# The last output tile of a two-block transformer layer: its second half shared by two engines

## The chip, the cores and the metric

The kernel runs on one core of a Trainium2 chip. A core has five engines that run their own instruction streams and meet only through semaphores: TensorE (PE, matrix products), VectorE (DVE, elementwise work), ScalarE (ACT, activations), GpSimd (POOL, elementwise work and its own DMA queue) and SyncE (SP, which here issues DMAs). Sixteen DMA engines move data between the core's memory (SBUF) and DRAM. The metric is the device time of one execution in microseconds (us); the median of several runs counts.

## The reference

Two transformer blocks follow each other on 512 tokens of 1024 channels. The change touches only the last lines of the second block: the product of the feed-forward network with its down matrix, its norm, and the residual.

```python
def rms_norm(x, g):
    xf = x.astype(jnp.float32)
    y = xf * lax.rsqrt(jnp.mean(xf * xf, axis=-1, keepdims=True) + RMS_EPS)
    return (y * g.astype(jnp.float32)).astype(x.dtype)
...
        f = jax.nn.gelu(u_gate, approximate=True) * u_val
        y = f @ w_down[layer].astype(f.dtype)
        x = x + rms_norm(y, norm_ffn_post[layer])
    return x
```

## The kernel before

Nearly all of the time goes into matrix products in three passes of split operands (`whi`, `wlo` for weights, `xh`, `xl` or `fh`, `fl` for activations). SyncE streams 270 weight pieces through four slots; ScalarE rounds each to `whi`, VectorE takes the rest `wlo`. The last phase, `down2`, computes its output by token rows: `QB` = 4 tiles of `P` = 128 tokens, each with two halves of `SEQ` = 512 channels, so that eight banks of PSUM hold tile t, half h at bank 2t+h. TensorE (`down_rows`, L745) runs the first 19 of the 22 weight pieces for all eight banks, and the last three bank by bank, so that the banks are finished one after another, about 2 us apart; each raises `rows_done`.

Behind TensorE stands a chain for each tile t:

- ScalarE (`rows_rooted`, L1174) squares a bank and sums the squares along a row into `row_sums`, and raises `rows_squared`. After the second half it takes the root of the mean (`row_root`, L1184).
- VectorE (`rows_out`, L1642) scales the first half's sum (`row_bias`, L1651), multiplies each bank by the gains into `gained` (L1653), inverts the root into `row_inv` (L1655), and finishes each half with one SCALAR_TENSOR_TENSOR (L1659): `gained * row_inv + res_rows`, where `res_rows` is the residual in row form. Each raises `rows_ready`. `step` counts a semaphore `vstep` at the end of an instruction, and `after_step` waits until all counted ones have ended.
- SyncE (L456 to L461) waits for each half in turn, stores it (256 KB), and at the end waits until all eight stores have landed (`stored`).

GpSimd has no part in this phase: its last work is a list of DMA issues that prepare `res_rows` and `gain_rows` (L520 to L527). All eight stores go through SyncE's queue. The order of all this is written out by hand.

Of the kernel before, what the change touches and what calls it, by code (L numbers as in the profile page):

```python
# [19 lines left out]
D = 1024  # L20
KD = D // P
SEQ = 512
# [15 lines left out]
QB = SEQ // P  # L38
# [123 lines left out]
KEPT_WHOLE = KFF - 3  # L162
TURN_ITS = (4, 5, 6, 7)
T_FROM = 18
BIAS_W = 384
STAT = 4
SUMS_AT = 496
# [15 lines left out]
def two_block_kernel(nc, x_in, w_in, vec_in, gain_in, dftc_in, dftp_in, onehot_in, rel_in, out):  # L183
    F32, F32R = mybir.dt.float32, mybir.dt.float32r
    ALU = mybir.AluOpType
# [4 lines left out]
    with ExitStack() as ctx:  # L190
        def sem(name):
            return ctx.enter_context(nc.semaphore(name))
# [42 lines left out]
        row_root = put("row_root", [P, QB])  # L235
        row_inv = put("row_inv", [P, QB])
# [37 lines left out]
        gained = put("gained", [P, QB, D], offset=x_at)  # L274
        turned = [put(f"turned{n}", [P, SEQ // 64, KD, 32], offset=big + (n * KFF + T_FROM) * SEQ * 4) for n in range(2)]
        res_rows = put("res_rows", [P, QB, 4, D // 4], offset=res_at)
# [106 lines left out]
        row_bias_ready = sem("row_bias_ready")  # L383
        row_root_ready = sem("row_root_ready")
        rows_ready = sem("rows_ready")

        def vec(name, n):
            return vecs[:, VCOL[name] + n:VCOL[name] + n + 1] if isinstance(n, int) else vecs[:, ds(n + VCOL[name], 1)]
# [50 lines left out]
        @block.sync  # L439
        def _(sp):  # L440
            sp.dma_start(vecs[:, 0:KD], vec_in[:, 0:KD]).then_inc(gain_landed, 16)
            for k in range(KD):
                sp.dma_start(res[:, k, :], x_in[:, k, :]).then_inc(x_landed[k], 16)
                if k % 2 == 0:
                    sp.dma_start(raw[:, k // 2, :], w_in[k // 2]).then_inc(w_landed[k // 2], 16)
            sp.dma_start(vecs[:, KD:], vec_in[:, KD:]).then_inc(vec_landed, 16)
            with sp.Fori(1, CHUNKS // SLOTS_W) as it:
                for s in range(SLOTS_W):

                    sp.wait_ge(w_used, it * SLOTS_W + (s - SLOTS_W + 1))  # L450
                    sp.dma_start(raw[:, s, :], w_in[ds(it * SLOTS_W + s, 1)].rearrange("a p c -> (a p) c")) \
                      .then_inc(w_landed[s], 16)
            for n in range(CHUNKS // SLOTS_W * SLOTS_W, CHUNKS):
                sp.wait_ge(w_used, n - SLOTS_W + 1)
                sp.dma_start(raw[:, n % SLOTS_W, :], w_in[n]).then_inc(w_landed[n % SLOTS_W], 16)
            for t in range(QB):  # L456
                for h in range(2):
                    sp.wait_ge(rows_ready, 2 * t + h + 1)
                    sp.dma_start(out[t, :, h * SEQ:(h + 1) * SEQ], gained[:, t, h * SEQ:(h + 1) * SEQ]) \
                      .then_inc(stored, 16)  # L460
            sp.wait_ge(stored, 32 * QB)  # L461


        @block.gpsimd
        def _(pool):
            pool.memset(ones[:, :], 1.0).then_inc(set_up, 1)
            pool.memset(ident[:, :], 0.0).then_inc(set_up, 1)
            pool.memset(folded[:, :, :, :], 0.0).then_inc(set_up, 1)
            pool.memset(cin1[:, :, 0:1], 0.0).then_inc(set_up, 1)
            pool.memset(cin1[:, :, N1 + 1:N1 + 2], 0.0).then_inc(set_up, 1)  # L470
            pool.memset(stage[:, :, N1:N1 + 2], 0.0).then_inc(set_up, 1)
            pool.memset(small[:, 2:3], RMS_EPS).then_inc(set_up, 1)
            pool.memset(small[:, 3:4], LN_EPS).then_inc(set_up, 1)
            pool.wait_ge(set_up, 2)
            pool.affine_select(out=ident[:, :], in_=ident[:, :], compare_op=ALU.not_equal, fill=1.0, base=0,
                               pattern=[[-1, P]], channel_multiplier=1).then_inc(set_up, 1)
            pool.wait_ge(x_landed[KD - 1], 16)
            pool.dma_start(onehot[:, :, :], onehot_in).then_inc(onehot_landed, 16)
            pool.dma_start(rel[:, :], rel_in).then_inc(onehot_landed, 16)

            pool.wait_ge(bias_copied, NG)
            for g in range(NG):
                pool.dma_start(bias_dram[g * HEADS:(g + 1) * HEADS, :],
                               bias_rows[g * HEADS:(g + 1) * HEADS, g, :]).then_inc(bias_stored, 16)
            pool.dma_start(dftp[0:ROWS, :, :, :], dftp_in).then_inc(dft_landed, 16)
            pool.dma_start(dftc, dftc_in).then_inc(dft_landed, 16)

            pool.wait_ge(bias_stored, 16 * NG)
            for n in range(NG * HEADS):
                if n:  # L490
                    pool.wait_ge(bias_spread, 16 * n)
                pool.dma_start(bias_copies[n], bass.AP(bias_dram.tensor, n * BIAS_W, [[0, P], [1, BIAS_W]])) \
                    .then_inc(bias_spread, 16)
            pool.wait_ge(bias_spread, 16 * NG * HEADS)

            def load_bias(j):

                for g in range(NG):
                    c0, c1 = ((0, 256), (256, 384), (384, 512))[g]
                    pool.dma_start(  # L500
                        bias[:, c0:c1],
                        bass.AP(bias_copies.tensor, (g * HEADS + j) * P * BIAS_W + P - 1,
                                [[BIAS_W - 1, P], [1, c1 - c0]])).then_inc(bias_landed, 16)

            for j in range(HEADS):
                if j:
                    pool.wait_ge(max_ready, 2 * j)
                else:
                    pool.wait_ge(operand_ready, READY["x2"])
                load_bias(j)  # L510
                pool.wait_ge(exp_ready, 8 * (j + 1))
                for kind in range(2):
                    pool.dma_start(stats_rows(kind == 0, 2 * SEQ * kind), head_stats[:, 0, 4 * kind:4 * kind + 4, :]) \
                        .then_inc(stats_stored, 16)
                pool.wait_ge(stats_stored, 32 * (j + 1))
                for kind in range(2):
                    pool.dma_start(head_stats[:, 1, 4 * kind:4 * kind + 4, :],
                                   stats_rows(kind == 0, 2 * SEQ * (1 - kind))).then_inc(stats_landed, 16)

            pool.wait_ge(res_turned, 2 * KD)  # L520
            for a in range(4):
                for u in range(4):
                    for n in range(2):
                        pool.dma_start(res_rows[32 * u:32 * (u + 1), 2 * n:2 * n + 2, a, :],
                                       turned[n][32 * a:32 * (a + 1), :, :, :]
                                       .rearrange("p (t u) c i -> p t u (c i)", u=4)[:, :, u]).then_inc(res_moved, 16)
            pool.dma_start(gain_rows[:, :], bass.AP(gain_in.tensor, 0, [[0, P], [1, D]])).then_inc(gain_spread, 16)  # L527


        @block.tensor  # L530
# [482 lines left out]
        def _(act):  # L1013
# [400 lines left out]
                          lambda k: xh2[:, k, :])  # L1414
            ffn_gelus("up2")
            rows_rooted("down2")


        @block.vector
        def _(dve):  # L1420
            steps = [0, 0]

            def step(instruction):
                instruction.then_inc(vstep, 1)
                steps[1] += 1

            def after_step():

                dve.wait_ge(vstep, steps[0] + steps[1])
# [212 lines left out]
            def rows_out():  # L1642
                for n in range(3, KFF):
                    w_to_lo("down2", 0, n)
                dve.wait_ge(gain_spread, 16)
                for t in range(QB):
                    for h in range(2):
                        cols = slice(h * SEQ, (h + 1) * SEQ)
                        dve.wait_ge(rows_squared, 2 * t + h + 1)
                        if h == 0:  # L1650
                            dve.tensor_scalar(row_bias[:, t:t + 1], row_sums[:, t, 0:1], 1.0 / D, RMS_EPS,  # L1651
                                              ALU.mult, ALU.add).then_inc(row_bias_ready, 1)
                        step(dve.tensor_tensor(gained[:, t, cols], ps[:, 2 * t + h, :], gain_rows[:, cols], ALU.mult))  # L1653
                    dve.wait_ge(row_root_ready, t + 1)
                    step(dve.reciprocal(row_inv[:, t:t + 1], row_root[:, t:t + 1]))  # L1655
                    after_step()
                    for h in range(2):
                        cols = slice(h * SEQ, (h + 1) * SEQ)
                        dve.scalar_tensor_tensor(out=gained[:, t, cols], in0=gained[:, t, cols],  # L1659
                                                 scalar=row_inv[:, t:t + 1],  # L1660
                                                 in1=res_rows[:, t, :, :].rearrange("p a n -> p (a n)")[:, cols],
                                                 op0=ALU.mult, op1=ALU.add).then_inc(rows_ready, 1)

            def down_sums(dn, name):
# [510 lines left out]
```

## Time and profile before

| what | us |
|---|---|
| median of 3 runs | 1582.26 |
| lowest and highest run | 1581.83, 1583.42 |
| the profiled execution | 1582.33 |
| its span, from first to last instruction | 1580.5 |
| TensorE busy in the span | 1570.8 |
| VectorE, ScalarE, GpSimd busy | 1103.5, 557.0, 47.3 |

The span is what the trace shows; the profiled execution's own time is 1.83 us longer. All times of single instructions are counted from the span's start. In the timeline a row gives start, duration, engine, line, operation, what it writes and reads, and in brackets how long the engine was idle before and who released it. Instructions of one engine can overlap by some hundredths of a microsecond, since the next may be taken in before the last has drained.

### The profile page before, as it was taken

The page shows a single profiled execution, that of the slowest core. Times are in us where ns is not written, and L with a number is a line of the kernel's source. Part 1 is how long each engine was busy: PE and PEld are TensorE (multiplying, and loading weights), DVE is VectorE, ACT ScalarE, POOL GpSimd, SP SyncE. Part 2 cuts the span into 40 slices and gives each one's busy share as a digit, 9 for nine tenths or more (in the row PEclk, how much of TensorE's full clock was granted, in tenths as well). Part 3 has the DMA queues.
Part 4 walks back from the last instruction along what each step waited for, and adds up shares of the span by engine and source line. Part 5 has one row for each costly group of instructions (what it writes and reads, how often), then busy time and mean ns, then how long its engine had stood idle before and what let it go on. Part 6 is the DMA issues. An engine that isn't in the chain of part 4 may idle for free.

```text
span 1580.5 us, 24351 instructions
## 1 busy us (share of the span) xinstructions
PE 1570.8 (99%) x9542; PEld 1417.9 (90%) x9542; DVE 1103.5 (70%) x1594; ACT 557.0 (35%) x809; POOL 47.3 (3%) x93
## 2 busy tenths in 40 slices
PE   9999999999999999999999999999999999999998
PEld 9999999999999988998889898888889888888887
DVE  6334456689888853278999898974656899988224
ACT  5123333542222222254234444458335422222112
POOL 1110000000000000000001010000000000040000
PEclk9999999999999999999999999999999999999999
DMA  5443222233333233333333232322332333363332
GB/s 175 115 137 93 87 70 86 79 95 93 93 93 88 87 105 107 94 103 92 101 99 87 80 101 74 94 82 80 96 102 70 107 94 98 101 159 93 102 98 93
DMA packets 44793, 154.18 MB, mean 98 GB/s; under 512 B 6346, under 2 KB 6374, under 8 KB 44720
## 3 DMA queue, kind: packets, MB, share of 16 engines
q1 hardware_dynamic: 41472, 146.21, 30.5%
q0 software_dynamic: 3248, 6.93, 2.0%
q8 instruction: 53, 0.87, 0.2%
q14 instruction: 20, 0.16, 0.0%
HBM read 148.88 MB, written 4.51 MB: 97 GB/s over the span
## 4 chain that ended last, share of the span: by engine, by line
PE 89%; DVE 8%; ACT 1%; DMA 1%; issue 1%; SPq 0%; DVEq 0%
PE ps L539 65%; PE ps L741 8%; PE ps L549 7%; PE ps L914 4%; DVE wlo L1444 2%; PE ps L577 1%; DVE work L1845 1%; DVE work L1570 1%; DVE work L1573 1%; PE ps L965 1%; DMA raw<-w_dram 1%; DVE work L1605 1%; DVE stage L1561 1%; PE ps L854 1%; DVE fl L1619 0%
## 5 line engine op out<-in xcount | busy, mean ns | idle before, releaser
L539 PE MATMUL ps<-xh,whi 128*128 128x258 f32 (+2 forms) x1800 | 495.2, 326 | 1.1 <-DVE stage L1566 0.8
L539 PE MATMUL ps<-xh,wlo 128*128 128x258 f32 (+2 forms) x1800 | 490.6, 323 | 0.0
L539 PE MATMUL ps<-xl,whi 128*128 128x258 f32 (+2 forms) x1800 | 489.9, 323 | 0.0
L1018 ACT ACTIVATE whi<-raw 128x1024 fp32r<-128x1024 f32 x270 | 285.3, 1058 | 476.4 <-DMA raw<-w_dram 454.7
L1444 DVE TENSOR_TENSOR wlo<-raw,whi 128x1024 fp32r<-128x1024 f32 x270 | 329.1, 1219 | 171.7 <-ACT whi L1018 171.1
L539 PEld LDWEIGHTS ps<-xh,whi 128*128 128x128 f32 x1800 | 301.5, 189 | 29.0 <-issue 3.4
L539 PEld LDWEIGHTS ps<-xh,wlo 128*128 128x128 f32 x1800 | 300.7, 189 | 27.1
L539 PEld LDWEIGHTS ps<-xl,whi 128*128 128x128 f32 x1800 | 301.4, 189 | 25.7 <-issue 0.2
L1845 DVE SCALAR_TENSOR_TENSOR work<-cin,vecs,work 128x512 f32<-128x512 f32 x240 | 180.1, 751 | 6.9
L1566 DVE TENSOR_TENSOR stage<-ps,rstd 128x516 f32<-128x516 f32 x57 | 39.5, 694 | 64.5 <-PE ps L539 62.2
L1573 DVE SCALAR_TENSOR_TENSOR work<-stage,vecs,work 128x512 f32<-128x512 f32 x88 | 66.2, 752 | 7.5 <-DVE work L1570 0.5
L1570 DVE SCALAR_TENSOR_TENSOR work<-stage,vecs,work 128x512 f32<-128x512 f32 x88 | 66.1, 752 | 7.5 <-DVE work L1605 0.5
L741 PE MATMUL ps<-whi,fl 128*128 128x512 f32 x176 | 68.5, 389 | 0.0
L741 PE MATMUL ps<-whi,fh 128*128 128x512 f32 x176 | 68.5, 389 | 0.0
L741 PE MATMUL ps<-wlo,fh 128*128 128x512 f32 x176 | 68.5, 389 | 0.0
L1144 ACT ACTIVATE work<-work 128x512 f32<-128x512 f32 x44 | 27.8, 631 | 103.4 <-DVE work L1573 103.2
L539 PE MATMUL ps<-fl,whi 128*128 128x512 f32 x132 | 51.4, 389 | 0.0
L539 PE MATMUL ps<-fh,wlo 128*128 128x512 f32 x132 | 51.4, 389 | 0.0
L539 PE MATMUL ps<-fh,whi 128*128 128x512 f32 x132 | 51.4, 389 | 0.0
L1605 DVE TENSOR_SCALAR work<-stage,vecs 128x512 f32<-128x512 f32 x88 | 47.7, 543 | 0.2
L549 PE MATMUL ps<-xh,whi 128*128 128x256 f32 (+1 forms) x160 | 45.9, 287 | 0.2 <-DVE xl L1480 0.2
L549 PE MATMUL ps<-xh,wlo 128*128 128x256 f32 (+1 forms) x160 | 45.2, 283 | 0.0
(255 smaller groups left out, 2292.4 us busy)
## 6 DMA issues: line engine op xcount, KB each, us to landing
raw<-w_dram SPq DMA_DIRECT2D x270, 512.0 KB, 3.5
bias_copies_dram<-bias_rows_dram POOLq DMA_DIRECT2D x12, 192.0 KB, 3.8
res<-x_dram SPq DMA_DIRECT2D x8, 264.0 KB, 6.2
res_rows<-turned POOLq DMA_DIRECT2D x32, 64.0 KB, 3.3
out_dram<-gained SPq DMA_DIRECT2D x8, 256.0 KB, 2.0
dftp<-dftp_dram POOLq DMA_DIRECT2D x1, 550.7 KB, 4.5
bias<-bias_copies_dram POOLq DMA_DIRECT2D x4, 128.0 KB, 2.8
bias<-bias_copies_dram POOLq DMA_DIRECT2D x8, 64.0 KB, 3.1
```

What stands on the lines that cost most here:

```text
L539: last = pe.matmul(ps[:, bank, 0:b - a], w[:, slot, cols], xx[:, k, a:b], start=start and n == 0, stop=stop and n == 2)
L549: last = pe.matmul(ps[:, bank, at_:at_ + b - a], w[:, slot, cols], xx[:, k, a:b], start=start and n == 0, stop=stop and n == 2)
L741: last = pe.matmul(ps[:, 2 * t + h, :], f[:, k, rows], w[:, slot, cols], start=k == k0 and n == 0, stop=k == k1 - 1 and n == 2)
L914: last = pe.matmul(ps[:, TILE_BANK[t], :], xx[:, 2 * c + k2, rows], w[:, n % 4, k2 * SEQ:(k2 + 1) * SEQ], start=c == 0 and k2 == 0 and m = ...
L1018: act.activation(whi[:, slot, :], raw[:, slot, :], ACT.Copy).then_inc(w_hi, 1)
L1144: act.activation(work[:, 1, 0:SEQ], work[:, 0, 0:SEQ], ACT.Gelu_apprx_tanh) \
L1444: dve.tensor_tensor(wlo[:, slot, :], raw[:, slot, :], whi[:, slot, :].bitcast(F32), ALU.subtract).then_inc(w_split, 1)
L1566: dve.tensor_tensor(halves(dst), tile_psum(slot, True), halves(by), ALU.mult).then_inc(tile_read, 1)
L1570: step(dve.scalar_tensor_tensor(out=dst, in0=src(at_, width), scalar=vec(w, tile), in1=dst, op0=ALU.mult, op1=ALU.add))
L1573: last(dve.scalar_tensor_tensor(out=dst, in0=src(at_ + 2, width), scalar=vec(w, tile + 2 * tiles), in1=dst, op0=ALU.mult, op1=ALU.add))
L1605: step(dve.tensor_scalar(row, stage[:, s, off + 1:off + 1 + SEQ], vec(w, m + (s * KFF + 2 * KFF)), vec(b, m + s * KFF), ALU.mult, ALU.add))
L1845: ins = dve.scalar_tensor_tensor(out=dst, in0=src, scalar=vec("conv_dw_w_2", t * KD + m), in1=dst, op0=ALU.mult, op1=ALU.add)
```

## The change

It concerns the last token tile (t = 3). Its second half, columns 512 to 1023, is cut at column 832. VectorE finishes the first half as before and then 320 columns. GpSimd finishes the last 192 (`TAIL_W`) in two instructions, a scaling by `row_inv` and an addition of `res_rows`. ScalarE's queue stores these 192 columns; SyncE stores seven halves and the 320 columns. Three semaphores are new: `tail_ready` (the reciprocal has ended), `tail_scaled` and `tail_added` (GpSimd's two steps).

```diff
+TAIL_W = 192
+STORES = [(t, h * SEQ, (h + 1) * SEQ) for t in range(QB) for h in range(2)][:-1] + \
+    [(QB - 1, SEQ, D - TAIL_W)]
...
-            for t in range(QB):
-                for h in range(2):
-                    sp.wait_ge(rows_ready, 2 * t + h + 1)
-                    sp.dma_start(out[t, :, h * SEQ:(h + 1) * SEQ], gained[:, t, h * SEQ:(h + 1) * SEQ]) \
-                      .then_inc(stored, 16)
-            sp.wait_ge(stored, 32 * QB)
+            for n, (t, a, b) in enumerate(STORES):
+                sp.wait_ge(rows_ready, n + 1)
+                sp.dma_start(out[t, :, a:b], gained[:, t, a:b]).then_inc(stored, 16)
+            sp.wait_ge(stored, 16 * len(STORES) + 16)
...
+            pool.wait_ge(tail_ready, 1)
+            t, last = QB - 1, slice(D - TAIL_W, D)
+            pool.tensor_scalar(gained[:, t, last], gained[:, t, last], row_inv[:, t:t + 1], None, ALU.mult) \
+                .then_inc(tail_scaled, 1)
+            pool.wait_ge(tail_scaled, 1)
+            pool.tensor_tensor(gained[:, t, last], gained[:, t, last],
+                               res_rows[:, t, :, :].rearrange("p a n -> p (a n)")[:, last], ALU.add) \
+                .then_inc(tail_added, 1)
...
             rows_rooted("down2")
+            act.wait_ge(tail_added, 1)
+            act.dma_start(out[QB - 1, :, D - TAIL_W:D], gained[:, QB - 1, D - TAIL_W:D]).then_inc(stored, 16)
...
                     dve.wait_ge(row_root_ready, t + 1)
-                    step(dve.reciprocal(row_inv[:, t:t + 1], row_root[:, t:t + 1]))
-                    after_step()
-                    for h in range(2):
-                        cols = slice(h * SEQ, (h + 1) * SEQ)
-                        dve.scalar_tensor_tensor(out=gained[:, t, cols], in0=gained[:, t, cols],
+                    if t == QB - 1:
+                        after_step()
+                        dve.reciprocal(row_inv[:, t:t + 1], row_root[:, t:t + 1]).then_inc(tail_ready, 1)
+                        dve.wait_ge(tail_ready, 1)
+                    else:
+                        step(dve.reciprocal(row_inv[:, t:t + 1], row_root[:, t:t + 1]))
+                        after_step()
+                    for _, a, b in [store for store in STORES if store[0] == t]:
+                        dve.scalar_tensor_tensor(out=gained[:, t, a:b], in0=gained[:, t, a:b],
                                                  scalar=row_inv[:, t:t + 1],
```

VectorE's last instructions before the change, the last tile's chain at the end of the program (each row: line, operation, output and inputs, shape, and the semaphores it waits for):

```order
L1651 TENSOR_SCALAR row_bias<-row_sums 128x1 [waits rows_squared]
L1653 TENSOR_TENSOR gained<-ps,gain_rows 128x512
L1653 TENSOR_TENSOR gained<-ps,gain_rows 128x512 [waits rows_squared]
L1655 RECIPROCAL row_inv<-row_root 128x1 [waits row_root_ready]
L1659 SCALAR_TENSOR_TENSOR gained<-gained,row_inv,res_rows 128x512 [waits vstep]
L1659 SCALAR_TENSOR_TENSOR gained<-gained,row_inv,res_rows 128x512
```

The same instructions with the change:

```order
L1665 TENSOR_SCALAR row_bias<-row_sums 128x1 [waits rows_squared]
L1667 TENSOR_TENSOR gained<-ps,gain_rows 128x512
L1667 TENSOR_TENSOR gained<-ps,gain_rows 128x512 [waits rows_squared]
L1671 RECIPROCAL row_inv<-row_root 128x1 [waits vstep,row_root_ready]
L1677 SCALAR_TENSOR_TENSOR gained<-gained,row_inv,res_rows 128x512 [waits tail_ready]
L1677 SCALAR_TENSOR_TENSOR gained<-gained,row_inv,res_rows 128x320
```

The wait on `vstep` has moved ahead of the reciprocal, the first half waits for `tail_ready`, and the last instruction has 320 columns.

GpSimd's last instructions with the change, behind its DMA issues (before, its program ends with the issue of `gain_rows`):

```order
L528 DMA res_rows<-turned_98 32x2x256
L528 DMA res_rows<-turned_99 32x2x256
L531 DMA gain_rows<-gain_dram 128x1024
L534 TENSOR_SCALAR gained<-gained,row_inv 128x192 [waits tail_ready]
L537 TENSOR_TENSOR gained<-gained,res_rows 128x192 [waits tail_scaled]
```

Two instructions are added at the end, each behind its own wait, and nothing on GpSimd is queued behind them.

## Rows read from the trace of the kernel before

**Rows 1.** The page: span, TensorE's busy time, the chain by engine.

```profile
span 1580.5 us, 24351 instructions
PE 1570.8 (99%) x9542; PEld 1417.9 (90%) x9542; DVE 1103.5 (70%) x1594; ACT 557.0 (35%) x809; POOL 47.3 (3%) x93
...
PE 89%; DVE 8%; ACT 1%; DMA 1%; issue 1%; SPq 0%; DVEq 0%
```

**Rows 2.** Timeline of the end: start, us, engine, line, operation, [idle before].

```profile
1574.75 0.39 PE L741 MATMUL ps<-wlo,fh 128*128 128x512 f32 x1
1575.17 0.60 ACT L1180 ACTIVATE sq<-ps 128x512 f32<-128x512 f32 x1 [1.35 <-PE ps L741]
1575.67 0.20 ACT L1180 ACTIVATION_READ_ACCUMULATOR sq<-ps 128x1 f32 x1
1575.89 0.29 ACT L1184 ACTIVATE row_root<-row_sums,row_bias 128x1 f32<-128x1 f32 x1
1575.89 0.69 DVE L1653 TENSOR_TENSOR gained<-ps,gain_rows 128x512 f32<-128x512 f32 x1 [1.21 <-ACT sq L1180]
1576.50 0.15 DVE L1655 RECIPROCAL row_inv<-row_root 128x1 f32<-128x1 f32 x1
1576.69 1.42 DVE L1659 SCALAR_TENSOR_TENSOR gained<-gained,row_inv,res_rows 128x512 f32<-128x512 f32 x2
```

**Rows 3.** Timeline of VectorE from 1577.5 on: the second half alone.

```profile
1577.36 0.75 DVE L1659 SCALAR_TENSOR_TENSOR gained<-gained,row_inv,res_rows 128x512 f32<-128x512 f32 x1
```

**Rows 4.** Timeline of SyncE's queue: issues of the last two stores.

```profile
1577.47 0.33 SPq L459 DMA_DIRECT2D out_dram<-gained  x1
...
1578.13 0.33 SPq L459 DMA_DIRECT2D out_dram<-gained  x1
```

**Rows 5.** The stores' line (ns of an issue, landing) and SyncE's last wait.

```profile
L459 SPq DMA_DIRECT2D out_dram<-gained x8: 332/333/344, 1565.2 to 1578.1; - x8
...
DMA to landing us min/median/max: 2.0/2.0/2.0
...
SPq L190 <- DMA out_dram<-gained: 1.7, 1, 1.7
```

**Rows 6.** Stretches: us, each engine's busy time, granted clock, DMA share, GB/s.

```profile
1578.20:1578.30 0.10, 0.00 (x0) 0.00 (x0) 0.00 (x0) 0.00 (x0) 0.00 (x0) 1.00 0.00 0
1578.30:1578.40 0.10, 0.00 (x0) 0.00 (x0) 0.00 (x0) 0.00 (x0) 0.00 (x0) 1.00 0.87 348
1578.90:1579.00 0.10, 0.00 (x0) 0.00 (x0) 0.00 (x0) 0.00 (x0) 0.00 (x0) 1.00 0.67 246
...
1579.70:1579.80 0.10, 0.00 (x0) 0.00 (x0) 0.00 (x0) 0.00 (x0) 0.00 (x0) 1.00 0.03 0
...
1578.20:1579.80 1.60, 0.00 (x0) 0.00 (x0) 0.00 (x0) 0.00 (x0) 0.00 (x0) 1.00 0.85 328
```

**Rows 7.** Groups on VectorE by shape: count, busy us, mean ns, idle before.

```profile
L1573 DVE SCALAR_TENSOR_TENSOR work<-stage,vecs,work 128x512 f32<-128x512 f32 x88 | 66.2, 752 | 7.5 <-DVE work L1570 0.5
...
L1480 DVE SCALAR_TENSOR_TENSOR xl<-res,vecs,xh 128x256 fp32r<-128x256 f32 x16 | 7.6, 477 | 0.4 <-ACT xh L1115 0.4
...
L1659 DVE SCALAR_TENSOR_TENSOR gained<-gained,row_inv,res_rows 128x512 f32<-128x512 f32 x8 | 5.7, 749 | 0.1
```

**Rows 8.** Timeline of GpSimd at the program's start.

```profile
0.25 0.10 POOL L2165 MEMSET const-float32-0.0<- 128x1 f32 x1 [0.25 <-issue]
...
0.75 0.20 POOL L466 MEMSET ones<- 128x128 f32 x1 [0.29 <-POOLq L2165]
...
2.98 0.10 POOL L473 MEMSET small<- 128x1 f32 x1
3.11 0.28 POOL L475 TENSOR_SCALAR_AFFINE_SELECT ident<-ident 128x128 f32<-128x128 f32 x1
```

**Rows 9.** GpSimd's issues; DMAs with KB and us to landing; a stretch of copies.

```profile
L524 POOL DMA_DIRECT2D res_rows<-turned x32 | 17.1, 544 | 347.3 <-DVE turned L1638 347.3
...
vecs<-vec_dram SPq DMA_DIRECT2D x1, 4.0 KB, 1.7
...
1399.00:1400.00 1.00, 1.00 (x7) 0.81 (x6) 0.96 (x3) 0.39 (x1) 1.00 (x3) 1.00 0.49 119
```

More of the change, by code:

```diff
@@ L385, in two_block_kernel @@
         rows_ready = sem("rows_ready")
+        tail_ready = sem("tail_ready")
+        tail_scaled = sem("tail_scaled")
+        tail_added = sem("tail_added")
         def vec(name, n):
@@ L1654, in rows_out @@
                     dve.wait_ge(row_root_ready, t + 1)
-                    step(dve.reciprocal(row_inv[:, t:t + 1], row_root[:, t:t + 1]))
-                    after_step()
-                    for h in range(2):
-                        cols = slice(h * SEQ, (h + 1) * SEQ)
-                        dve.scalar_tensor_tensor(out=gained[:, t, cols], in0=gained[:, t, cols],
+                    if t == QB - 1:
[7 more added lines that the diff above has]
+                        dve.scalar_tensor_tensor(out=gained[:, t, a:b], in0=gained[:, t, a:b],
                                                  scalar=row_inv[:, t:t + 1],
-                                                 in1=res_rows[:, t, :, :].rearrange("p a n -> p (a n)")[:, cols],
+                                                 in1=res_rows[:, t, :, :].rearrange("p a n -> p (a n)")[:, a:b],
                                                  op0=ALU.mult, op1=ALU.add).then_inc(rows_ready, 1)
```

## The prediction

> **What bounds the kernel now.** I began with the page's busy line and its chain [rows 1]: TensorE is busy for 1570.8 of 1580.5 us and carries 89% of the chain that ended last. The change touches none of its instructions and nothing before the last token tile. So the question is only what happens after the last matmul, and I read that stretch from the timeline [rows 2]. The last matmul is started at 1574.75 and ScalarE's square of the last bank starts at 1575.17. VectorE then multiplies the last bank by the gains (1575.89, 0.69 us), inverts the root (1576.50, 0.15 us), and finishes the two halves with two SCALAR_TENSOR_TENSOR, the first from 1576.69, the second from 1577.36 [rows 3]. SyncE issues the store of the first half at 1577.47 and that of the second at 1578.13 [rows 4]; each lands 2.0 us after its issue, and the last wait is 1.7 us for a store [rows 5]. The span closes at 1580.5.
>
> The view that decides is the stretch of the stores [rows 6]. The DMA engines are idle until 1578.3, 0.83 us after the first issue. They are then close to full until 1579.7: over 1.6 us they are busy 0.85, which is 1.36 us of work, inside 1.4 us of wall time. The share dips once, to 0.67 at 1578.9, where the second store takes over from the first. Each store is thus about 0.68 us of work for all engines, and the second begins when the first is drained, which happens to be 0.84 us after its own issue (1578.13 + 0.84 = 1578.97). Two limits lie on each other here: VectorE's second half, and the drain of 512 KB, which starts with the first half's store. Shortening VectorE's second half alone moves only the first of the two.
>
> **The scale.** The span's 1580.5 us belong to a run of 1582.33 us, 1.83 us outside the span; that run lies 0.07 us over the median of 1582.26 us. The runs are spread over 1.6 us. About 0.2%, 3.2 us, is what a measurement of this kernel can tell from no change. Everything from the end of the reciprocal (1576.65) to the end of the span is 3.85 us, and the part that the change rewrites, the two halves on VectorE, is 1.42 us of it. No outcome of the sharing itself can be a gain of 3.2 us.
>
> **The change, part by part.** First, the reciprocal of the last tile now waits for VectorE's own last product. Before, it started at 1576.50, ahead of the product's end at 1575.89 + 0.69 = 1576.58 [rows 2]. Behind this wait on VectorE stand the reciprocal and both halves; SyncE and GpSimd wait for those. A step behind a wait on its predecessor starts 0.04 us after it here (reciprocal ends at 1576.65, the half starts at 1576.69), so the reciprocal starts at 1576.62, 0.12 us later. The other bound is the convolution's chain of such steps, 7.5 us of idle time before 88 of them [rows 7], 0.085 us each: 1576.67, 0.17 us later. I take 0.12, since its row is the same place. The first half then starts at 1576.81 and ends at 1577.56, and its store is issued at 1577.59 in place of 1577.47.
>
> Second, VectorE's second half shrinks from 512 to 320 columns. The same instruction takes 749 ns with 512 columns and 477 ns with 256 [rows 7], or 1.06 ns per column; 320 columns give 477 + 64 x 1.06 = 545 ns, 204 ns less. It starts, as before, 0.08 us ahead of the end of the first (1577.48) and ends at 1578.02, where 1578.11 stood. VectorE's gain is thus 0.20 - 0.12 = 0.08 us. SyncE's issue of the first store ends at 1577.59 + 0.33 = 1577.92, ahead of this, so the queue is no limit; the second store is issued at 1578.05.
>
> Third, GpSimd takes 192 columns in two instructions, a scaling and an addition, each behind a semaphore. The trace of before has no such instruction. The nearest rows are its memsets, 98 ns with 1 column and 205 ns with 128, and its select, which reads and writes 128 columns, 282 ns [rows 8]. By the memset a column costs 0.84 ns, so 192 cost 0.26 us; by the select 1.45 ns, so 0.38 us. That bounds the scaling. The addition reads two tensors: its lower bound is the select's 0.38 us, its upper bound twice the select's price per column, 0.66 us. Between dependent instructions GpSimd shows 0.03 us (3.08 to 3.11). So from tail_ready at 1576.77: start 1576.80, end between 1577.5 and 1577.9. The row that it is nearest to is the select, so I take the upper half, 1577.8. None of it lies on the path yet: VectorE's halves run until 1578.02 beside it, and the next point says how long the cover holds.
>
> Fourth, ScalarE issues the 96 KB of those columns. Its last work, the root, ends at 1576.18; nothing is queued behind its wait. An issue takes 0.33 us on SyncE [rows 5] and 0.54 us on GpSimd's queue [rows 9], and the data start 0.83 us after the start of an issue: with the columns ready at 1577.8, about 1578.7. The engines are then still draining the first store, from 1578.42 to 1579.10. The other two stores are 160 KB and 96 KB, 0.42 and 0.25 us of work. If the 160 KB go first, the 96 KB are needed at 1579.52, so ScalarE may issue as late as 1578.69 before the end moves. This is GpSimd's cover: 0.9 us beyond my 1577.8, and 0.8 us beyond its upper bound.
>
> Fifth, the drain. The bytes are the same 512 KB, and their start is 0.12 us later. A single queue's two stores already keep the engines full [rows 6]; no row shows two hardware queues storing at once. The Trainium skill's page "DMA: Bandwidth & Descriptors", section "Issuing engines are not separate DMA queues", states that DMAs of any issuing engine end on the same 16 DMA engines, and that several issuers only save issue time; by it the drain stays 1.36 us of work, and were it otherwise the 0.25 us of the tail store could be hidden. The rows give the same choice without it: full engines have nothing to give. What is dearer is that each row of 2 KB now leaves in two pieces, 1280 and 768 bytes. From below this costs nothing: work in proportion to bytes. From above, a stretch in which mostly 1 KB pieces move (64 KB copies between tiles) runs at 119 GB/s with a share of 0.49 [rows 9], 243 GB/s if full, 67 ns a piece, against 328/0.85 = 386 GB/s and 85 ns for a 2 KB piece of the stores. A straight line through both gives 62 and 71 ns for the two pieces, 48 ns more per row, and with 128 rows on 16 engines 8 x 48 ns = 0.38 us. Those copies go between tiles and through another queue, while the stores are their own nearest row, so I take 0.10 us, nearer to the lower bound.
>
> **The sum.** End of drain: 1579.70 + 0.12 + 0.10 = 1579.92; receipt and close as before, so the span is 1580.7 and the run 1582.33 + 0.22 = 1582.55. Taken back to the median (0.07) this is 1582.5 us. With the bounds, +0.10 to +0.55: 1582.4 to 1582.8. This is no change that can be measured.
>
> **Rival one: GpSimd and VectorE take turns, slower.** Both halves on VectorE read two tensors in SBUF, and both GpSimd instructions read SBUF. No row shows the two engines so at the same time. If they exclude each other, their times add up whatever the order: on VectorE 1.21 us for both halves, on GpSimd 0.26 to 0.38 and 0.38 to 0.66 us, with three handovers of 0.03 us, 1.95 to 2.35 us from 1576.81, so the last of them ends at 1578.75 to 1579.15. If GpSimd's addition is last, ScalarE issues 0.1 to 0.5 us after the latest harmless time, 1578.69. If GpSimd goes first, the first half's store starts 0.26 to 0.38 us later, and the drain with it. Added to the forecast's 0.22, this is 0.3 to 0.7 us, middle 0.5: 1582.8 us. It decides from the point at which GpSimd's sum is finished after 1578.69. The Trainium skill's page "SBUF — State Buffer", section "Who interferes with whom", states this exclusion for a VectorE instruction with two SBUF inputs against a GpSimd instruction that reads SBUF, as a lock held for the whole instruction. Against it stands no row, for it none either: its chance is 0.32.
>
> **Rival two: the last issue is the limit, faster.** All eight stores land 2.0 us after issue, the last of a pair as well as the first [rows 5], and 4 KB on the same queue land in 1.7 us [rows 9]. If landing goes by the issue and the size of the last store, not by the drain, then SyncE's last store (issued at 1578.05, 0.08 us earlier) lands between 0.08 and 0.38 us earlier, middle 0.25: 1582.0 us. The full engines of rows 6 speak against it. Chance 0.14.
>
> **Rival three: something is paid once, slower.** GpSimd does its first arithmetic since 3.1 us into the span, and ScalarE's queue its first transfer. GpSimd's first instruction stands 0.25 us after the start, its select follows the memset by 0.03 us [rows 8], and SyncE's first transfers show no price of this kind. So by rows it is 0 to 0.25 us, hidden in GpSimd's cover of 0.9. It shows in the time only from 0.9 us on, and in a measurement only from some 4 us on. The Trainium skill's page "GPSIMD Engine Reference", section "Instruction dispatch", gives about 6 us for the first call of a freshly loaded kernel; were that due here, the estimate would be 1582.5 + 5 = 1587.5 us. Chance 0.04.
>
> **How the numbers follow.** Forecast 1582.5 us with 0.50, rival one 1582.8 with 0.32, rival two 1582.0 with 0.14, rival three with 0.04. The first three are all within 3.2 us of the median, so "same" gets 0.95; a little under the third rival, 0.04, goes to slower and 0.01 to faster, for which the profile has no mechanism. The range leaves out rival three and the outer part of the others. The cases' own bounds run from 1581.9 to 1583.0; the spread of the runs, 1581.83 to 1583.42, adds about half a microsecond on either side: 1581.4 to 1583.6.
>
> **What would show it.** In the timeline after: the reciprocal right behind the product (1576.62 in the times of before), not ahead of its end; a half of 320 columns at about 0.545 us; GpSimd's two instructions, whose lengths and place beside VectorE's halves tell the forecast from rival one (stretched halves, or GpSimd idle until a half ends, show exclusion). In the DMA windows: a start 0.12 us later relative to the last matmul, and 1.36 to 1.75 us of work. If the last transfer to land is ScalarE's, GpSimd's cover was too small. The forecast is wrong if the close of the span follows the last issue by less than before, or if a run differs by more than 3 us, which would mean a cost that these rows do not hold.

## The result, and the profile after

The changed kernel takes 1587.70 us (median of 7 runs, 1587.15 to 1589.47) against 1582.26 us before: the ratio is 1.0035, 95% interval 1.0025 to 1.0045. It is slower by 5.4 us, and the prediction of 1582.5 us, in a range to 1583.6, was wrong.

The loss is all behind VectorE's last product. The page's head, and the timeline from VectorE's last product on (columns as in [rows 2]):

```profile
span 1585.8 us, 24355 instructions
PE 1569.7 (99%) x9542; PEld 1416.6 (89%) x9542; DVE 1103.7 (70%) x1594; ACT 557.2 (35%) x809; POOL 49.5 (3%) x95
...
1575.91 0.69 DVE L1667 TENSOR_TENSOR gained<-ps,gain_rows 128x512 f32<-128x512 f32 x1 [1.20 <-ACT sq L1192]
1576.70 0.16 DVE L1671 RECIPROCAL row_inv<-row_root 128x1 f32<-128x1 f32 x1
1576.90 1.38 DVE L1677 SCALAR_TENSOR_TENSOR gained<-gained,row_inv,res_rows 128x512 f32<-128x512 f32 x2
1576.97 1.32 POOL L534 TENSOR_SCALAR gained<-gained,row_inv 128x192 f32<-128x192 f32 x1 [161.56 <-DVE row_inv L1671]
1577.68 0.96 SPq L464 DMA_DIRECT2D out_dram<-gained  x2
1578.38 0.59 POOL L537 TENSOR_TENSOR gained<-gained,res_rows 128x192 f32<-128x192 f32 x1
1579.00 0.37 ACTq L1430 DMA_DIRECT2D out_dram<-gained  x1
```

VectorE's last product starts at 1575.91 where 1575.89 stood [rows 2], so up to there nothing has changed. From there to the end of the span it was 4.61 us; now it is 9.89 us. The last issue, ScalarE's, is at 1579.00, and its 96 KB land 1.8 us later, at 1580.8. Five more microseconds pass in which this timeline shows nothing.

They are seen in the rows of the program's end. Line 193 (190 before) is the `with` under which all engines' programs stand; each engine's closing steps carry its number. Some of these rows, first before, then after (x and count, ns of one as minimum/median/maximum, first and last start):

```profile
L190 POOLq DRAIN  x1: 10122/10122/10122, 1412.8 to 1412.8; - x1
L190 SPq COMPARE_BRANCH  x1: 38/38/38, 1580.2 to 1580.2; - x1
L190 SPq DRAIN  x1: 7/7/7, 1580.3 to 1580.3; - x1
```

```profile
L193 POOLq EVENT_SEMAPHORE  x2: 17/17/17, 1585.6 to 1585.7; - x2
...
L193 DVEq DRAIN  x1: 1420/1420/1420, 1576.9 to 1576.9; - x1
L193 POOLq DRAIN  x1: 7257/7257/7257, 1578.3 to 1578.3; - x1
L193 ACTq DRAIN  x1: 147/147/147, 1579.4 to 1579.4; - x1
L193 SPq COMPARE_BRANCH  x1: 38/38/38, 1580.8 to 1580.8; - x1
L193 SPq DRAIN  x1: 7/7/7, 1581.0 to 1581.0; - x1
L193 SPq EVENT_SEMAPHORE  x1: 17/17/17, 1585.8 to 1585.8; - x1
```

Each engine closes its program with an instruction that the trace names DRAIN, and then the engines meet at semaphores. GpSimd's DRAIN takes microseconds. Before, GpSimd reached its end behind its DMA issues at 1412.8 and its 10.1 us lay under the products of the last weights. Now it begins when the addition has been started (1578.34, the last piece of the chain of work below), lasts 7.26 us to 1585.6, and the program ends right behind it. SyncE's waits show the same from the other side (us in total, times, longest); before, its wait on line 190 for the meeting was 0.2 us:

```profile
1576.97 1.32 POOL gained L534
1578.29 0.04 issue
1578.34 0.63 POOLq L193
...
SPq L193 <- PEq L193: 4.8, 1, 4.8
SPq L193 <- DMA out_dram<-gained: 2.1, 1, 2.1
```

So of the 5.3 us in the trace, 0.6 us are a later last landing (SyncE's DRAIN starts at 1580.96, before at 1580.32, which the rows round to tenths: 5.05 us behind the product's start, 4.42 before) and 4.6 us are SyncE's longer wait for the meeting. The waits name PE, which was long done (its own drain began at 1570.9); the one late engine among the closing rows is GpSimd.

### The profile page after: what moved, and what is told of

It reads as the page before. It is cut to its first block, busy times and chain, and to the rows that moved or that the text cites. A ratio compares the mean times of both kernels' runs of the same rounds, so it can differ in the third digit from the quotient of the medians.

```text
span 1585.8 us, 24355 instructions
## 1 busy us (share of the span) xinstructions
PE 1569.7 (99%) x9542; PEld 1416.6 (89%) x9542; DVE 1103.7 (70%) x1594; ACT 557.2 (35%) x809; POOL 49.5 (3%) x95
## 4 chain that ended last, share of the span: by engine, by line
PE 89%; DVE 8%; ACT 1%; DMA 1%; issue 1%; POOL 0%; SPq 0%; POOLq 0%; DVEq 0%
PE ps L551 65%; PE ps L753 8%; PE ps L561 7%; PE ps L926 4%; DVE wlo L1458 2%; PE ps L589 1%; DVE work L1863 1%; DVE work L1584 1%; DVE work L1587 1%; PE ps L977 1%; DMA raw<-w_dram 1%; DVE work L1619 1%; DVE stage L1575 1%; PE ps L866 1%; DVE fl L1633 0%
## 5 line engine op out<-in xcount | busy, mean ns | idle before, releaser
L561 PE MATMUL ps<-xl,whi 128*128 128x256 f32 (+1 forms) x160 | 45.2, 283 | 0.0
```

The costliest lines, as they stand in the source:

```text
L561: last = pe.matmul(ps[:, bank, at_:at_ + b - a], w[:, slot, cols], xx[:, k, a:b], start=start and n == 0, stop=stop and n == 2)
```

## Experiments

The theory after the result: GpSimd's closing drain has a length of its own, counted from the end of its work, and whatever makes GpSimd reach its end late puts that length on the path. Its rivals: ScalarE's queue, used for the first time, closes late; or a price is paid once, by GpSimd's first arithmetic.

**Without GpSimd's part.** VectorE does the 192 columns itself, ScalarE still stores them.

```diff
-            pool.wait_ge(tail_ready, 1)
-            pool.tensor_scalar(gained[:, t, last], ...).then_inc(tail_scaled, 1)
-            pool.wait_ge(tail_scaled, 1)
-            pool.tensor_tensor(gained[:, t, last], ...).then_inc(tail_added, 1)
...
+                    if t == QB - 1:
+                        a, b = D - TAIL_W, D
+                        dve.scalar_tensor_tensor(...).then_inc(tail_added, 1)
```

> GpSimd's two instructions are taken out; VectorE finishes the 192 columns itself with a third instruction, and ScalarE's queue still stores them. Theory A (GpSimd's closing drain, 7.26 us in the changed kernel, is the loss): the drain is back at 1413 us, hidden, and what is left is the later reciprocal and one more VectorE instruction (192 columns, about 0.33 us on the path): span 1580.8 us, time 1582.6. Rival (ScalarE's queue, used for the first time, is what closes late): span stays at 1585 us.

Measured: 1582.60 us, ratio 1.0003 (0.9994 to 1.0013). Closing rows, and VectorE's parts alone:

```profile
L193 POOLq DRAIN  x1: 10239/10239/10239, 1412.5 to 1412.5; - x1
L193 ACTq DRAIN  x1: 147/147/147, 1578.6 to 1578.6; - x1
...
1577.28 0.55 DVE L1669 SCALAR_TENSOR_TENSOR gained<-gained,row_inv,res_rows 128x320 f32<-128x320 f32 x1
1577.74 0.41 DVE L1675 SCALAR_TENSOR_TENSOR gained<-gained,row_inv,res_rows 128x192 f32<-128x192 f32 x1
```

GpSimd's drain is back under the products and the 5 us are gone, while ScalarE's queue is still in use and drains in 0.15 us. The queue is not the cause.

**The same work once before.** The changed kernel, with GpSimd's two kinds of instruction run on scratch at 1415 us.

```diff
+            pool.memset(scr[:, :], 1.0).then_inc(warm, 1)
+            pool.wait_ge(warm, 1)
+            pool.tensor_scalar(scr[:, 8:200], scr[:, 8:200], scr[:, 0:1], None, ALU.mult).then_inc(warm, 1)
+            pool.wait_ge(warm, 2)
+            pool.tensor_tensor(scr[:, 8:200], scr[:, 8:200], scr[:, 8:200], ALU.add).then_inc(warm, 1)
             pool.wait_ge(tail_ready, 1)
```

> The changed kernel, with a memset and the same two kinds of GpSimd instruction (192 columns, on scratch) once before, behind GpSimd's last DMA issue at 1415 us. Theory A1 (the drain has this length behind any late GpSimd work): span 1585.8, time 1587.7, as in the changed kernel. Rival A2 (a price paid once, by the first arithmetic): the drain at the end is short, span about 1581.2 us, time 1583.

Measured: 1587.88 us, ratio 1.0034 (1.0021 to 1.0047), and GpSimd's rows, with the instruction that VectorE ran beside the first use:

```profile
1414.99 0.75 DVE L1594 SCALAR_TENSOR_TENSOR work<-stage,vecs,work 128x512 f32<-128x512 f32 x1
1415.20 1.18 POOL L536 TENSOR_SCALAR scr<-scr 128x192 f32<-128x192 f32 x1
...
1576.36 1.32 POOL L541 TENSOR_SCALAR gained<-gained,row_inv 128x192 f32<-128x192 f32 x1 [159.40 <-DVE row_inv L1678]
...
L193 POOLq DRAIN  x1: 7255/7255/7255, 1577.7 to 1577.7; - x1
```

The scaling takes 1.32 us when it is the second of its kind, as it did in the changed kernel where it was the first: no price of the first use shows. (The first one here, 1.18 us, has VectorE beside it too and ends 0.64 us behind VectorE's instruction; what that means is read below.) The drain is 7.26 us again. Nothing of the loss is paid once.

**A bare wait.** The kernel without GpSimd's part, but GpSimd waits at its end for the last reciprocal, with no instruction behind it.

```diff
+            pool.wait_ge(tail_ready, 1)
```

> x1_no_gpsimd with a bare wait of GpSimd for the reciprocal of the last tile, and no instruction behind it. If the drain has a fixed length from the moment GpSimd reaches its end, it runs from 1576.9 for 6.6 to 7.3 us: span 1583.7 to 1584.4, time 1585.5 to 1586.2. If it is long only behind instructions that GpSimd has just run: span 1580.8 us, time 1582.6.

**One memset.** The same with a memset of one column behind the wait.

```diff
+            pool.wait_ge(tail_ready, 1)
+            pool.memset(scr[:, 0:1], 1.0)
```

> x3_wait_only with one memset of 128x1 on GpSimd behind the wait (a kind that it ran at the start, 0.1 us, no input). Drain behind any instruction: ends 6.6 us after the memset's end at 1577.1, span 1583.9, time 1585.7. Drain long only behind instructions that read SBUF, or behind first arithmetic: span 1580.8 us, time 1582.6.

Measured: 1585.99 us (ratio 1.0024, 1.0014 to 1.0033) with the bare wait, 1585.77 us (1.0023, 1.0013 to 1.0032) with the memset. The drain of the first, SyncE's wait in it, and the drain of the second:

```profile
L193 POOLq DRAIN  x1: 6602/6602/6602, 1577.2 to 1577.2; - x1
...
SPq L193 <- PEq L193: 3.2, 1, 3.2
```

```profile
1577.96 0.10 POOL L534 MEMSET scr<- 128x1 f32 x1 [161.28 <-DVE row_inv L1666]
...
L193 POOLq DRAIN  x1: 6727/6727/6727, 1577.9 to 1577.9; - x1
```

A wait alone is enough, although GpSimd had rested for 161 us. The drain is 6.60 us with nothing ahead of it; behind the memset 6.73, which is the memset's 0.10 and 6.6; in the changed kernel 7.26, which is 0.63 us until the addition has ended (1578.34 to 1578.97) and 6.63. The length of 6.6 us is the same behind a bare wait, a memset and the addition.

**The same bare wait, 3.5 us earlier.** GpSimd waits for the first finished half of tile 2 in place of the last reciprocal.

```diff
+            pool.wait_ge(rows_ready, 5)
```

> x3_wait_only, with GpSimd's bare wait moved from the last tile's reciprocal to the first finished half of the tile before (some 3.5 us earlier, at 1573.4). If the drain is 6.6 us from the moment GpSimd reaches its end, it ends at 1580.0 to 1580.1, just ahead of the last store's landing: span 1580.6 to 1580.9, time 1582.5, against 1585.99 in x3_wait_only. If a late wait of any kind costs, the time stays over 1584.

Measured: 1582.78 us (ratio 1.0002, 0.9992 to 1.0011).

```profile
L193 POOLq DRAIN  x1: 6602/6602/6602, 1573.1 to 1573.1; - x1
...
SPq L193 <- PEq L193: 0.2, 1, 0.2
```

The drain has the same 6.60 us, and now it ends at 1579.7, ahead of the last landing. What counts is when GpSimd comes to its end.

**The sharing, at another tile.** GpSimd takes the last 192 columns of tile 1 in place of tile 3, by the same instructions.

```diff
+TAIL_T = 1
...
-            t, last = QB - 1, slice(D - TAIL_W, D)
+            t, last = TAIL_T, slice(D - TAIL_W, D)
...
-                    if t == QB - 1:
+                    if t == TAIL_T:
```

> The changed kernel's sharing, applied to the second token tile (t = 1) in place of the last: the same GpSimd instructions and the same cut, some 8 us before the end; ScalarE's store of its 192 columns goes out behind its last root. GpSimd ends at about 1570.5, its drain at 1577.1, hidden. Theory A: time 1582.3 (1582.0 to 1582.8), span 1580.5. Rival (sharing itself costs some us, wherever it stands): over 1585.

Measured: 1582.88 us, ratio 1.0003 (0.9993 to 1.0012).

```profile
1569.03 1.32 POOL L534 TENSOR_SCALAR gained<-gained,row_inv 128x192 f32<-128x192 f32 x1 [153.40 <-DVE row_inv L1671]
1570.43 0.60 POOL L537 TENSOR_TENSOR gained<-gained,res_rows 128x192 f32<-128x192 f32 x1
...
L193 POOLq DRAIN  x1: 7267/7267/7267, 1570.4 to 1570.4; - x1
```

The work is the same to 0.01 us, the drain too, and the time is within the interval of no change: it is not the sharing that costs, but that it stands less than 6.6 us from the end.

**How the two engines meet at SBUF.** In the changed kernel GpSimd's scaling takes 1.32 us and ends (1578.29) with VectorE's second part (1578.28). Two more kernels ran once each; they are read for their rows, not for their times. First GpSimd's part was put behind VectorE altogether:

```diff
             pool.wait_ge(tail_ready, 1)
+            pool.wait_ge(rows_ready, 2 * QB)
```

> The changed kernel, but GpSimd also waits until VectorE has finished both parts of the last tile, so that the two never run side by side. Theory A (the engines take turns at SBUF beside each other): the scaling, 1.32 us in the changed kernel, falls to 0.26 to 0.5 us, and VectorE's 320 columns, 0.71 us there, to 0.55 us. Rival (GpSimd's scaling simply takes that long): 1.2 to 1.3 us again. Either way the drain starts late: span 1585.5 to 1586.5 us.

Then VectorE's two parts were exchanged, 320 columns first:

```diff
-STORES = [...][:-1] + [(QB - 1, SEQ, D - TAIL_W)]
+STORES = [...][:-2] + [(QB - 1, SEQ, D - TAIL_W), (QB - 1, 0, SEQ)]
```

> The changed kernel with VectorE's two parts of the last tile in the other order: 320 columns first, then 512, GpSimd's scaling beside them as before. It tells how the two engines get in each other's way. If GpSimd waits until VectorE's first instruction has ended and then runs beside the second: its scaling ends some 0.2 us earlier, 1.12 us long instead of 1.32, and VectorE's second instruction (512 columns) is the longer one by 0.16 us, 0.91 us. If GpSimd waits for both: its scaling ends with VectorE's last, 1.32 us or more, and the 512 columns take 0.75. If both are only slowed throughout: 1.32 us, and either part is longer. The close is not touched: drain 7.26 us, span 1585.5 to 1586.

Measured, with GpSimd behind VectorE:

```profile
1576.91 0.55 DVE L1678 SCALAR_TENSOR_TENSOR gained<-gained,row_inv,res_rows 128x320 f32<-128x320 f32 x1
...
1577.65 0.77 POOL L535 TENSOR_SCALAR gained<-gained,row_inv 128x192 f32<-128x192 f32 x1 [162.83 <-DVE gained L1678]
1578.50 0.59 POOL L538 TENSOR_TENSOR gained<-gained,res_rows 128x192 f32<-128x192 f32 x1
```

and with the parts exchanged:

```profile
1576.88 1.12 POOL L534 TENSOR_SCALAR gained<-gained,row_inv 128x192 f32<-128x192 f32 x1 [161.57 <-DVE row_inv L1671]
...
1577.28 0.91 DVE L1677 SCALAR_TENSOR_TENSOR gained<-gained,row_inv,res_rows 128x512 f32<-128x512 f32 x1
```

Alone the scaling takes 0.77 us. That lies between what the two theories of that run expected (0.26 to 0.5 us, and 1.2 to 1.3), and is 0.55 us less than beside VectorE. With the short part first it loses 0.35 us, 0.20 less, which is the 0.20 us by which VectorE's first instruction is shorter; and the instruction that is slowed, by 0.16 us, is VectorE's second in both orders (712 ns for 547 with 320 columns, 912 for 749 with 512). In both orders, and at the first use in the warmed kernel, GpSimd's scaling ends 0.63 to 0.64 us behind the end of the VectorE instruction that ran when it started. So these rows read as GpSimd waiting for VectorE's first instruction and then taking 0.16 us from the second. They do not fit a lock for whole instructions in both directions: on that reading VectorE's second part would have waited for most of GpSimd's 0.64 us. Both runs closed late, as expected (spans 1586.0 and 1585.5 us).

**Three pieces on VectorE.** The kernel before, with the last tile in parts of 384, 384 and 256 columns and the middle one on ScalarE's queue.

```diff
+LAST = ((0, 384), (384, 768), (768, D))
...
+                    for a, b in LAST if t == QB - 1 else ((0, SEQ), (SEQ, D)):
```

> The kernel before, without GpSimd, the last tile finished by VectorE in three pieces of 384, 384 and 256 columns in place of two halves, the middle one stored by ScalarE's queue. The first store is issued 0.14 us earlier (384 columns by 1.06 ns and the rest: 0.61 us for 0.75), the last part ends 0.1 us later. By the drain, which starts 0.14 us earlier and has the same bytes: 0.1 to 0.2 us less than before, 1582.1; by the last issue: 0.1 us more. Either is within what the runs can tell; the trace from the last product (1575.89) to the span's end, 4.61 us before, shows which.

Measured: 1582.49 us, ratio 1.0003 (0.9994 to 1.0012).

```profile
span 1580.2 us, 24353 instructions
1575.31 0.69 DVE L1661 TENSOR_TENSOR gained<-ps,gain_rows 128x512 f32<-128x512 f32 x1 [1.20 <-ACT sq L1185]
...
1577.68 0.33 SPq L465 DMA_DIRECT2D out_dram<-gained  x1
...
1577.50:1577.60 0.10, 0.00 (x0) 0.00 (x0) 0.10 (x1) 0.00 (x0) 0.00 (x0) 1.00 0.08 31
1579.10:1579.20 0.10, 0.00 (x0) 0.00 (x0) 0.00 (x0) 0.00 (x0) 0.00 (x0) 1.00 0.12 31
1579.20:1579.30 0.10, 0.00 (x0) 0.00 (x0) 0.00 (x0) 0.00 (x0) 0.00 (x0) 1.00 0.00 0
```

From the last product to the end of the span it is 4.84 us, before 4.64 (spans unrounded; the printed tenths would give 4.89 and 4.61). That is 0.2 us more, although the first store went out 1.45 us behind the product (1576.76) where it had been 1.58. The data (columns as in [rows 6]) also start earlier, and they end at the same place, 3.9 us behind the product here and before [rows 6]. The last issue is 2.37 us behind the product, before 2.24 [rows 4], and that store lands in 2.1 us, before 2.0. So in this one trace the end follows the last issue, not the start or the end of the data.

No run found a version faster than the kernel before.

## Why the prediction was wrong, point by point

**The step that failed is the third point, GpSimd's part.** It asked who waits for GpSimd's result, found ScalarE's store and a cover of 0.9 us, and put none of GpSimd's time on the path. It left out what stands behind GpSimd's last instruction: the end of its program, for which all engines wait. The row was in the trace of before (L190, 10.1 us at 1412.8), under the same line number as SyncE's last wait, which I did read [rows 5]. In its place the runs showed 6.6 us from GpSimd's last instruction, or bare wait, to the meeting; 1578.97 + 6.6 = 1585.6, and the span ends at 1585.8. The statement that no outcome of the sharing can reach 3.2 us holds for a gain only, as it was put; the loss had no such bound, and the low chance that I gave it rested on what I had looked at.

**Rival three had nearly the time (1587.5 us) by luck.** It put a one-off price ahead of GpSimd's first arithmetic. The warmed kernel (1587.88 us) shows no one-off price, and the wait alone (1585.99 us) shows that arithmetic is not needed. The 6 us that the Trainium skill's page "GPSIMD Engine Reference", section "Instruction dispatch", gives for the first call of a freshly loaded kernel do not show in these runs: the time lies behind the work, each time.

**The reciprocal's wait.** For this 0.12 us was taken, and 0.17 was the upper bound; the reciprocal now starts 0.79 us behind the product's start, before 0.61: 0.18 us.

**VectorE's parts.** 545 ns for 320 columns was right (545 to 547 ns where GpSimd does nothing beside it). Beside GpSimd it is 712 ns, so that VectorE's gain of 0.08 us became a loss: its last part ends 2.37 us behind the product's start, before 2.22.

**GpSimd's own time.** The addition, 0.38 to 0.66 us, is 0.59. The scaling, 0.26 to 0.38 us from memset and select [rows 8], is 0.77 us alone and 1.32 beside VectorE: two bounds from instructions without a scalar operand did not bound it.

**The cover, in the fourth point, did not hold either.** GpSimd's result was ready at 1578.97 in place of 1577.8, and ScalarE issued at 1579.00, behind the 1578.69 that the prediction gave as the latest harmless time. The stretches show the cost: SyncE's two stores are through by 1579.7, and ScalarE's 96 KB follow by themselves.

```profile
1579.60:1579.70 0.10, 0.00 (x0) 0.00 (x0) 0.00 (x0) 0.00 (x0) 0.00 (x0) 0.50 0.33 103
1579.70:1579.80 0.10, 0.00 (x0) 0.00 (x0) 0.00 (x0) 0.00 (x0) 0.00 (x0) 0.50 0.01 0
1579.90:1580.00 0.10, 0.00 (x0) 0.00 (x0) 0.00 (x0) 0.00 (x0) 0.00 (x0) 0.50 0.78 269
1580.20:1580.30 0.10, 0.00 (x0) 0.00 (x0) 0.00 (x0) 0.00 (x0) 0.00 (x0) 0.50 0.15 39
...
1578.50:1580.35 1.85, 0.00 (x0) 0.00 (x0) 0.00 (x0) 0.00 (x0) 0.46 (x1) 0.50 0.77 284
```

This is the 0.6 us by which the last landing is later. Without the closing drain the change would, as an estimate, have taken 1582.26 + 0.6 = 1582.9 us, inside the stated range. The price of the smaller pieces, taken as 0.10 us, was about right: the DMA engines' work is 1.85 us by 0.77, 1.42 us, before 1.36.

**Rival one, the turns.** The mechanism is there, smaller and mostly on one side: 0.55 us on GpSimd and 0.16 on VectorE. It expected a loss of 0.3 to 0.7 us, and the later last landing is 0.6 us; in part that is luck, since GpSimd's scaling is 0.77 us by itself, where this rival counted 0.38 at most. The Trainium skill's page "SBUF — State Buffer", section "Who interferes with whom", says that these two contend and calls the shared port pair an exclusive lock. GpSimd's wait agrees; a lock that GpSimd then holds against VectorE's next instruction for all of its own is not what 0.16 us shows, and the measurement decides.

**The drain of the DMA engines, and rival two.** The forecast let the last landing follow the start of the first store. The three pieces speak for rival two's reading, the last issue plus 1.8 to 2.1 us, and the kernel without GpSimd (issue 1578.18, landing 2.0 us later) fits it too. These are single traces and tenths of a microsecond, so this is likely and not shown. That rival forecast a gain since it took VectorE's last part to end earlier and SyncE's store, not ScalarE's, to be the last.

What stays open: why GpSimd's drain takes 6.6 us. Behind its DMA issues it took 10.1 us, some 7.5 us from the end of the last issue (1415.4) to 1422.9. There it was not constant: 10.2 us without GpSimd's part and 9.7 us in the kernel with three pieces. Whether the 6.6 us depend on GpSimd's having issued DMAs in this program was not tried.

## What to carry to other kernels

Before work is moved to an engine near the end, read what every engine does after its last instruction: the closing rows come onto the path when that engine reaches its end too late to hide them. On GpSimd they were 6.6 us here, so it had to be at its end, waits included, that much before the last store lands; work that it does earlier is free of this, as the sharing at tile 1 showed. And when a trace's last microseconds show no instruction, ask for the line of the enclosing block.

## What the runs showed of the hardware

- GpSimd's closing DRAIN is 6.60 us behind a bare wait after 161 us of rest, and 6.6 us from the end of a memset or an addition; ScalarE's is 0.15 us behind a DMA issue.
- GpSimd scales 192 columns by a per-partition value in 0.77 us and adds two tensors of that width in 0.59 us: the operation with one tensor was the slower one.
- GpSimd's scaling, which reads SBUF, ended 0.63 to 0.64 us behind the end of a VectorE instruction with two SBUF inputs that ran when it started, whether that was 512 or 320 columns long, and cost VectorE's next one 0.16 us, with 320 or with 512 columns.
